# Two decoder blocks in one kernel: the program's first loads and last stores cut into pieces

## The reference

```python
def rms_norm(x, g):
    xf = x.astype(jnp.float32)
    y = xf * lax.rsqrt(jnp.mean(xf * xf, axis=-1, keepdims=True) + NORM_EPS)
    return (y * g.astype(jnp.float32)).astype(x.dtype)

def swiglu(x, w1, w2):
    gu = x @ w1
    g, u = gu[..., :D_FF], gu[..., D_FF:]          # D_FF = 2816
    return (jax.nn.silu(g) * u) @ w2

x = x + 0.5 * swiglu(rms_norm(x, ffn1_norm[0]), ffn1_w1[0], ffn1_w2[0])   # the first phase
...
h = h + swiglu_2(rmsnorm(h, ffn_norm[1]), ffn_w_gu[1], ffn_w_down[1])     # the last feed-forward
return rmsnorm(h, final_norm)                                             # the last norm
```

## Time and profile before

| | |
|---|---|
| Median of 3 runs | 2128.18 us (2127.81 to 2129.77) |
| Profiled execution: device time, span of its instructions | 2129.35 us, 2127.5 us |
| PE busy | 2040.4 us (96%) |
| DVE, ACT, POOL busy | 1236.3 us (58%), 1008.9 us (47%), 239.9 us (11%) |
| HBM traffic | 354 MB, mean 166 GB/s |
| Chain that ended last | PE 80%, DVE 9%, ACT 4% |

### The profile page before, as it was taken

The page is one execution under the profiler, slowest core; times in us unless marked ns, Lnnn a source line. Parts: engine busy times, 40 slices in busy tenths (PEclk is TensorE's granted clock), DMA queues, the critical chain, the costliest instruction groups (busy, mean ns, idle before and its releaser), DMA issues.

```text
span 2127.5 us, 26438 instructions
## 1 busy us (share of the span) xinstructions
PE 2040.4 (96%) x9866; PEld 1683.7 (79%) x9866; DVE 1236.3 (58%) x1361; ACT 1008.9 (47%) x1270; POOL 239.9 (11%) x354
## 2 busy tenths in 40 slices
PE   6999988999999999988999999999999999999997
PEld 5888876778888888876778887778778888788886
DVE  4545659965545545659965555555555545446453
ACT  4344664445445344664445444544545344454442
POOL 1000069000000000069000002111100000000000
PEclk9999998999999999998999999999999999999999
DMA  6554532455555554542455554444435554415552
GB/s 221 202 192 170 196 142 85 166 183 181 194 179 185 201 193 169 197 142 87 164 183 191 195 179 158 145 145 145 139 119 186 189 193 163 158 60 208 187 187 79
DMA packets 53617, 354.14 MB, mean 166 GB/s; under 512 B 7584, under 2 KB 8224, under 8 KB 11680
## 3 DMA queue, kind: packets, MB, share of 16 engines
q1 hardware_dynamic: 53536, 353.04, 46.7%
HBM read 351.97 MB, written 1.05 MB: 166 GB/s over the span
## 4 chain that ended last, share of the span: by engine, by line
PE 80%; DVE 9%; ACT 4%; DVEq 2%; issue 2%; POOL 1%; POOLq 1%; DMA 1%; ACTq 0%; SPq 0%
PE psum L1706 56%; PE psum L1757 17%; DVE wlo L972 3%; DVE arena L1160 2%; ACT whi L545 2%; DVEq L1154 2%; PE psum L1774 1%; PE psum L1830 1%; PE psum L2122 1%; PE psum L2143 1%; DMA raw<-w_stream 1%; PE psum L2129 1%; PE psum L1718 1%; PE psum L1878 0%; DVE arena L1171 0%
## 5 line engine op out<-in xcount | busy, mean ns | idle before, releaser
L972 DVE TENSOR_TENSOR wlo<-raw,whi 128x2048 fp32r<-128x2048 f32 x325 | 744.1, 2292 | 448.3 <-ACT whi L545 447.9
L1706 PE MATMUL psum<-whi,xTh 128*128 128x512 f32 (+1 forms) x1936 | 769.1, 397 | 22.2 <-DVE xTl L979 11.6
L1706 PE MATMUL psum<-wlo,xTh 128*128 128x512 f32 (+1 forms) x1936 | 753.3, 389 | 0.0
L1706 PE MATMUL psum<-whi,xTl 128*128 128x512 f32 (+1 forms) x1936 | 753.1, 389 | 0.0
L545 ACT ACTIVATE whi<-raw 128x2048 fp32r<-128x2048 f32 x325 | 621.1, 1916 | 264.2 <-PE psum L1757 151.3
L1706 PEld LDWEIGHTS psum<-whi,xTh 128*128 128x128 f32 x1936 | 367.0, 190 | 100.0 <-DVE wlo L1529 10.3
L1706 PEld LDWEIGHTS psum<-whi,xTl 128*128 128x128 f32 x1936 | 367.0, 190 | 76.4
L1706 PEld LDWEIGHTS psum<-wlo,xTh 128*128 128x128 f32 x1936 | 367.7, 190 | 69.4
L1757 PE MATMUL psum<-whi,braT 128*128 128x512 f32 x1056 | 337.8, 390 | 1.0 <-DVE braT L1098 1.0
L1757 PEld LDWEIGHTS psum<-whi,braT 128*128 128x128 f32 x1056 | 198.3, 188 | 42.4 <-DVE braT L1098 1.3
L1757 PE MATMUL psum<-wlo,braT 128*128 128x512 f32 x528 | 205.5, 389 | 0.0
(11 more groups left out here) (227 smaller groups left out, 1482.2 us busy)
## 6 DMA issues: line engine op xcount, KB each, us to landing
raw<-w_stream SPq DMA_DIRECT2D x327, 1024.0 KB, 4.8
bias<-chunks SPq DMA_DIRECT2D x18, 256.0 KB, 5.0
x<-x_in SPq DMA_DIRECT2D x1, 1024.0 KB, 5.1
arena<-gate_w SPq DMA_DIRECT2D x2, 512.0 KB, 5.3
arena<-fins SPq DMA_DIRECT2D x2, 512.0 KB, 5.8
out<-x SPq DMA_DIRECT2D x1, 1024.0 KB, 4.0
con<-consts SPq DMA_DIRECT2D x1, 720.0 KB, 11.9
vec<-vecs SPq DMA_DIRECT2D x2, 94.5 KB, 4.4
```

Source lines behind the costliest of these rows:

```text
L972: TT(wlo[:, r], raw[:, r], whi[:, r].bitcast(F32), ALU.subtract).then_inc(lo_done, 1)
L1706: ins = pe.matmul(dst(rb), s(kt)[:, rows], w[:, r, at_:at_ + cols], start=start and n == 0 and k == 0, stop=stop and n == len(kts) - 1 and ...
```

## The change

The diff has two halves.

At the start: SP no longer issues the positions and the gain; ACT issues them on its own queue, as its first two instructions. x is loaded in two column halves, slot 0 in four quarters of 512 columns, with its own semaphore each, in the order first constants, x half 0, quarter 0, x half 1, quarters 1 to 3, slot 1, slot 2. ACT copies (`first_hi`) and DVE subtracts (`first_lo`) quarter by quarter, and `norm_hi` and `norm_lo` of the first tiles stand behind the first quarter. PE waits for slot 0 quarter by quarter. The two sines on ACT stand behind the silu of unit 0 in the first feed-forward. POOL makes the bf16 masks after the first norm factors instead of before.

At the end: the last feed-forward also runs `last_units`, in an order of its own that completes row block 0 first. DVE adds row block 0's quarters, multiplies x by the final gain into `d_x` at once, then does row block 1. ACT squares quarter by quarter, POOL makes the factor of one row block at a time, and the last scaling is one multiply by a per-token factor: the left half of each row block on ACT, which also stores it, the right half on DVE, stored by SP. The output leaves in four stores.

```diff
@@ sync @@
-            sp.dma_start(posi[:], positions).then_inc(pos_in, 16)
+            def x_half(c):
+                sp.dma_start(x[:, :, c * W:(c + 1) * W], x_in.rearrange("(r p) c -> p r c", p=P)[:, :, c * W:(c + 1) * W]).then_inc(x_loaded[c], 16)
+            def first_piece(n):
+                sp.dma_start(raw[:, 0, n * W:(n + 1) * W], w_stream[0, :, n * W:(n + 1) * W]).then_inc(piece_in[n], 16)
             sp.dma_start(con[:, 0:FIRST], consts[:, 0:FIRST]).then_inc(con_in, 16)
-            sp.dma_start(x[:], x_in.rearrange("(r p) c -> p r c", p=P)).then_inc(x_loaded, 16)
-            sp.dma_start(gain[:], gains[0]).then_inc(gain_in, 16)
-            for s in range(3):
+            x_half(0)
+            first_piece(0)
+            x_half(1)
+            for n in range(1, 4):
+                first_piece(n)
+            for s in range(1, 3):
                 sp.dma_start(raw[:, s], w_stream[s]).then_inc(loaded[s], 16)
...
-            sp.wait_ge(x_done, phases[-1][1].x + 8)
-            sp.dma_start(out.rearrange("(r p) c -> p r c", p=P), x[:]).then_inc(stored, 16)
-            sp.wait_ge(stored, 16)
+            for rb in range(RB):
+                sp.wait_ge(out_dve, rb + 1)
+                sp.dma_start(out[rb * P:(rb + 1) * P, W:], x[:, rb, W:]).then_inc(stored, 16)
+            sp.wait_ge(stored, 16 * 2 * RB)
@@ scalar @@
+            def first_hi(n):
+                act.wait_ge(piece_in[n], 16)
+                ins = act.activation(whi[:, 0, n * W:(n + 1) * W], raw[:, 0, n * W:(n + 1) * W], ACT.Copy)
+                if n == 3:
+                    ins.then_inc(hi_done, 1)
+                else:
+                    ins.then_inc(piece_hi, 1)
...
             def ffn(b):
                 if not b.early:
+                    first_hi(0)
                     norm_hi(b, 0)
+                    for n in range(1, 4):
+                        first_hi(n)
+                    act.wait_ge(loaded[1], 16)
+                    act.activation(whi[:, 1], raw[:, 1], ACT.Copy).then_inc(hi_done, 1)
                 norm_hi(b, 1)
...
                 silu(0)
+                if not b.early:
+                    act.wait_ge(trig_pool, 1)
+                    act.activation(msin[:], ang[:, 0].rearrange("p (r n) -> p r n", r=RB), ACT.Sin)
+                    act.activation(mcos[:], ang[:, 1].rearrange("p (r n) -> p r n", r=RB), ACT.Sin).then_inc(trig_act, 1)
                 with act.Fori(1, UNITS - 1) as j:
...
-            act.wait_ge(trig_pool, 1)
-            act.activation(msin[:], ang[:, 0].rearrange("p (r n) -> p r n", r=RB), ACT.Sin)
-            act.activation(mcos[:], ang[:, 1].rearrange("p (r n) -> p r n", r=RB), ACT.Sin).then_inc(trig_act, 1)
-            for s in range(2):
-                act.wait_ge(loaded[s], 16)
-                act.activation(whi[:, s], raw[:, s], ACT.Copy).then_inc(hi_done, 1)
+            def fin(b):
+                def square(rb, c):
+                    act.wait_ge(x_done, b.x + 2 * rb + c + 1)
+                    n = 2 * rb + c
+                    ins = act.activation(junk[:, 0:W], x[:, rb, c * W:(c + 1) * W], ACT.Square, accum_out=ss8[:, n:n + 1])
+                    if c:
+                        ins.then_inc(ss_done, 1)
+                    act.drain()
+                def out_left(rb):
+                    act.wait_ge(r_done, b.norm + rb + 1)
+                    act.wait_ge(xg_done, 4 + 2 * rb + 2)
+                    act.activation(x[:, rb, 0:W], d_x[:, rb, 0:W], ACT.Copy, scale=rs[:, rb:rb + 1]).then_inc(out_act, 1)
+                    act.wait_ge(out_act, rb + 1)
+                    act.dma_start(out[rb * P:(rb + 1) * P, 0:W], x[:, rb, 0:W]).then_inc(stored, 16)
+                square(0, 0)
+                square(0, 1)
+                square(1, 0)
+                out_left(0)
+                square(1, 1)
+                out_left(1)
+            act.dma_start(posi[:], positions).then_inc(pos_in, 16)
+            act.dma_start(gain[:], gains[0]).then_inc(gain_in, 16)
@@ vector @@
             def ffn(b):
                 if not b.early:
+                    first_lo(0)
                     norm_lo(b, 0)
+                    dve.wait_ge(x_loaded[1], 16)
+                    dve.sem_inc(x_done, 2)
+                    for n in range(1, 4):
+                        first_lo(n)
+                    dve.wait_ge(hi_done, 2)
+                    TT(wlo[:, 1], raw[:, 1], whi[:, 1].bitcast(F32), ALU.subtract).then_inc(lo_done, 1)
                 norm_lo(b, 1)
...
+                def last_rows(c, rb):
+                    dve.drain()
+                    cols = slice(c * W, (c + 1) * W)
+                    TT(d_x[:, rb, cols], x[:, rb, cols], gfin[:, cols], ALU.mult).then_inc(xg_done, 1)
+                if not b.next:
+                    dve.wait_ge(fin_in, 32)
+                    residual(0, b.ffn_scale, ready, ((0, 0), (1, 0)))
+                    last_rows(0, 0)
+                    last_rows(1, 0)
+                    for c in range(2):
+                        residual(0, b.ffn_scale, ready, ((c, 1),))
+                        last_rows(c, 1)
+                    return
...
             def fin(b):
-                dve.wait_ge(r_done, b.norm + 1)
-                dve.wait_ge(fin_in, 32)
-                for c in range(2):
-                    for rb in range(RB):
-                        xs = x[:, rb, c * W:(c + 1) * W]
-                        STT(xs, xs, rs[:, rb:rb + 1], gfin[:, c * W:(c + 1) * W], ALU.mult, ALU.mult).then_inc(x_done, 1)
+                for rb in range(RB):
+                    dve.wait_ge(r_done, b.norm + rb + 1)
+                    dve.drain()
+                    TS(x[:, rb, W:], d_x[:, rb, W:], rs[:, rb:rb + 1], None, ALU.mult).then_inc(out_dve, 1)
@@ gpsimd @@
+            def fin(b):
+                for rb in range(RB):
+                    wait(ss_done, b.norm * 2 + rb + 1)
+                    r = rs[:, rb:rb + 1]
+                    TT(r, ss8[:, 2 * rb:2 * rb + 1], ss8[:, 2 * rb + 1:2 * rb + 2], ALU.add)
+                    pool.drain()
+                    TS(r, r, 1.0 / D, EPS, ALU.mult, ALU.add)
+                    pool.drain()
+                    TT(r, r, mhalf[:, 0:1], ALU.pow).then_inc(r_done, 1)
@@ tensor: use @@
-                pe.wait_ge(lo_done, b.slot + more + (i + 1))
+                first = isinstance(i, int) and isinstance(more, int) and b.slot + more + i == 0
+                if not first:
+                    pe.wait_ge(lo_done, b.slot + more + (i + 1))
                 for n, (kt, at_) in enumerate(kts):
+                    if first and n < 3:
+                        pe.wait_ge(piece_lo, n + 1)
+                    elif first:
+                        pe.wait_ge(lo_done, 1)
@@ tensor: last_units @@
+                    if not b.next:
+                        down_block(before, j - 1, 0, 0)
+                        down_block(before, j - 1, 1, 0)
+                        pe.wait_ge(h_row, b.ffn * UNITS + UNITS)
+                        turn_h(j)
+                        down_block(before, j - 1, 0, 1)
+                        down_block(last, j, 0, 0, stop=True).then_inc(ffn_out, 1)
+                        down_block(last, j, 1, 0, stop=True).then_inc(ffn_out, 1)
+                        down_block(before, j - 1, 1, 1).then_inc(slot_used, 1)
+                        down_block(last, j, 0, 1, stop=True).then_inc(ffn_out, 1)
+                        down_block(last, j, 1, 1, stop=True).then_inc(slot_used, 1)
+                        return
```

More of the change, by code:

```diff
@@ L382, in h_of @@
         def h_of(b, j, part):
-            t0 = 2 if b.next and isinstance(j, int) and j == UNITS - 1 else 0
+            t0 = 2 if isinstance(j, int) and j == UNITS - 1 else 0
             return braT[:, part, t0:t0 + 2]
@@ L1759, in down_block, with down @@
                     return ins
-                def down(i, j, more=0, first=False, last=False):
+                def down(i, j, more=0, first=False):
                     for c in range(2):
                         for rb in range(RB):
-                            ins = down_block(i, j, c, rb, more, first, last)
-                            if last and not (c == 1 and rb == 1):
-                                ins.then_inc(ffn_out, 1)
+                            ins = down_block(i, j, c, rb, more, first)
                     ins.then_inc(slot_used, 1)
@@ L1809, in ffn @@
                 unit(1, first=True)
-                with pe.Fori(2, UNITS - 1 if b.next else UNITS) as j:
+                with pe.Fori(2, UNITS - 1) as j:
                     unit(j)
-                if b.next:
-                    last_units()
-                else:
-                    pe.wait_ge(h_row, b.ffn * UNITS + UNITS)
-                    turn_h(UNITS - 1)
-                    down(3 * UNITS - 1, UNITS - 1, last=True)
+                last_units()
             def turn(b, plan, name, parts, at_=None):
```

44 lines of the change are left out of this document (29 added, 15 removed).

## The result

The changed kernel takes 2112.84 us (median of 6 runs, 2112.17 to 2114.13); the kernel before, run beside it, 2128.19 us (6 runs, 2127.51 to 2129.77). The ratio is 0.9927, 95% interval 0.9917 to 0.9938: 15.35 us less, where 15.7 and 2112.5 us were forecast. The profiled execution took 2112.89 us with a span of 2111.1; that is its kernel's median, while the profiled execution before (2129.35 us, granted clock 0.980) stands 1.16 above its own.

A forecast was written before the change was run, and what follows sets the result against it. The prediction saw a long run of matmuls on PE with two uncovered ends. Start 10.5 plus end 5.2 gave 15.7 us, so 2128.18 - 15.7 = 2112.5 us, range 2108.0 to 2119.2.

The forecast's parts named there:

- the start: From the kernel's start to the first matmul on slot 2: gain 10.5 us, bounds 7 and 12.5.
- the end: Last unit, final norm and stores: gain 5.2 us, bounds 3.5 and 6.2.
- The mark: First matmul on slot 2, after which every unit repeats: forecast to move from 33.98 to 23.5 us.
- the two chains: Two paths to the first matmul on slot 2: PE's own at 23.5, slot 1 and 2 splits at 23.2; a tie.
- POOL's masks and the tables are wanted by the mixer near 200 us: nothing: POOL's mask casts and the sine tables in the first feed-forward: moving them later was priced at nothing.
- The sines: Two sines moved behind ACT's first silu: priced at nothing; without the cover of ACT's idle time, 1.3 us a unit.
- The reload rival: Uncovered table reload in the first feed-forward's loop: 1.28 us in each of nine passes, 11.5 in all, 2124.0 us; chance 0.04.
- The low clock: PE's first matmuls at the start: twelve at 1.2 GHz, 0.42 us apart, 5.1 us.
- Twelve matmuls less at the low clock would give 2.4 more: Bound on the start: twelve fewer slow matmuls on PE give 2.4 us, twelve more take 2.4.
- Serial fixed cost: Loads at the start: six pieces each add 2 us before the next, slot 1 8 us later, 2120.5 us; chance 0.05.
- Late clock: Waits between pieces keep PE at 1.2 GHz through slots 0 and 1: 7.2 us lost, 2119.7 us; chance 0.08.
- Slower: Low clock continues past the start; 79 more slow matmuls eat the gain, two units give 2141 us; chance 0.03.

The follow-up runs named there:

- start_only: The changed kernel with the norm, the last unit and the store put back as they were before: 2118.9 us, ratio 0.9955.
- masks_late: The changed kernel with GpSimd's mask casts moved to the head of the mixer's program; they ran at the same time as before: 2112.68 us.
- warm: The changed kernel with small fp32 products on TensorE while it waits, eight before the first transposes and four behind: 2116.66 us, ratio 0.9947.
- all_five: The changed kernel with the edits of `order`, `warm` and `masks_mixer`, and the last square ahead of the left half: 2111.12 us, ratio 0.9918.
- order: The changed kernel with slot 1 split in halves, slot 2's split ahead of the squares, second turned rows ahead of slot 1: 2112.13 us, ratio 0.9922.
- end_only: The kernel before with only the norm, last unit and store as in the changed kernel: 2122.14 us, ratio 0.9973.
- sines_first: The changed kernel with the two sines put back ahead of the first quarter on ScalarE: 2119.32 us, ratio 0.9956.
- masks_mixer: The changed kernel with GpSimd's two casts moved into the first mixer, behind its first waits: 2113.78 us, ratio 0.9933.
- whole_loads: The changed kernel with x and slot 0 each loaded by one DMA, work still in quarters: 2115.45 us, ratio 0.9937.

## Why the prediction was right, and where its terms were off

The mechanism held: two uncovered ends, independent of each other, the middle untouched. The total was within 0.4 us of the measured one, and that is in part luck: the start gave 1.15 us less than forecast, the end 0.8 more.

**The start: 9.35 us, 10.5 forecast.** The mark was forecast at 23.5 with the two chains tied at 23.5 and 23.2. They are still nearly tied (24.40 and 24.59), 0.9 and 1.4 us later. Arrivals: x half 0 at 5.2 (5.4 forecast), quarter 0 at 6.7 (6.2), x half 1 at 8.3 (7.9), quarter 1 at 9.85 (8.7), the last quarter at 11.1 (10.4), slot 1 at 13.66 (13.0). What was mis-sized is the transfer of the pieces in the middle: 314 GB/s were taken from a stretch of 0.19 MB, and the queue moved 235 between 5.20 and 6.70 us and over 400 from 8.3 on. Slot 1 then came 2.5 us behind the last quarter, as forecast (2.6). SyncE's slow issues are not the cause: in `start_only` its three issues of quarters took 2.47 us instead of 1.71 and slot 1 was issued at 5.14 instead of 4.38, and yet it landed earlier, at 13.08.

On TensorE's side the first matmul was at 9.14 (8.7), and tile 4 at 18.85 (18.0), by slot 1's lateness; 24 matmuls take it to 24.40.

On the data side slot 1's 0.66 and the cast's 0.94 come to 1.6, and 0.2 less for the copies and squares (5.74 us from slot 1's landing to slot 2's split; 5.95 summed). The cast is the mis-priced step: "POOL's masks and the tables are wanted by the mixer near 200 us: nothing" is true of who waits for their result, and false of who shares their time. In the kernel before the casts ran at 16.77 and 18.38, long before slot 2's split, and its low parts at 31.43 took 4.50 for two. The exclusion could have been read there already, from the other side: the identity's cast took 1.65 us beside VectorE's low part (0.29 us in `masks_late`, with VectorE idle). The bounds of the start, 7 and 12.5 us, have no working of their own: the 2.4 us either way that stand before them would give 8.1 and 12.9.

**The sines: nothing, as priced.** The reload rival is out: silu's table serves the sines too (from 24.64 to the mixer's at 206.49 there is no load), so no 1.28 us falls into any unit.

**The low clock: twelve matmuls, as forecast.** But the step "Twelve matmuls less at the low clock would give 2.4 more" was wrong as a statement on this kernel. With them alone taken away the mark came 1.4 us later (`warm`). With the data chain freed as well it came 3.1 earlier (`all_five`), where the data chain alone had given 0.8 (`order`). That difference, 2.3, is close to the 2.4, but it is there only once the other chain is out of the way. A bound worked out for one of two tied chains isn't a bound for the kernel.

**The end: 5.96 us, 5.2 forecast.** Last residual 1.26 us sooner behind the last up projection (1.06 worked out). From it to the last store's issue 4.27 us (4.3), with the last square 0.65 late behind the left quarter and its issue (0.5). From that issue to the span's end 2.92 us, where 3.5 was taken: ScalarE's last quarter landed in 2.5 us, not in 3.1; the first one, alone in the queue for most of its time, in 2.0, and both of SyncE's in 2.0. So the two last stores cost each other 0.5 us at most. (Of the blocks of the unit before, two lie behind the last `turn_h`, not three as the prediction says; its sum uses only the one that follows at once.)

**The middle: nothing.** The 1.1 us by which the two traces differ there are what single executions vary by, and the forecast had set that apart (1.17 us between the profiled execution and the median). From the mark to silu's table load near 1600 us, where all kernels do the same work but for sines and casts, the fourteen traces take 1577.1 to 1580.8 us: the kernel before 1578.9, `end_only`, with the same start, 1580.0, the changed kernel 1577.9. They follow no order of how early the mark is. The 1.8 us of `sines_first` and much of what `all_five` lost lie within this.

**The rivals.** Serial fixed cost: out, slot 1 landed 0.7 us later than forecast, not 8. Late clock: out here, though `warm` shows the thing itself, with a wait of 2.29 us behind a full clock. Slower: no sign of it.

## What to carry to other kernels

Where two chains arrive together, price an edit by both: removing a cost from one gives only what the other is behind, and a faster TensorE can pay its gain back in clock by waiting longer (here 2.29 us of waiting, eight matmuls at half speed). When an instruction is moved because "nobody wants its result", look at what runs beside it at its new place. And a difference of one or two microseconds between two single traces of 2100 is not yet an effect: the same 1580 us of work varied by 3.7 here, so hold it against the medians before you explain it.

## What the runs showed of the hardware that was not expected

- VectorE's fp32 subtraction of two SBUF operands and GpSimd's cast from SBUF take turns by whole instructions: 3.23 us instead of 2.29 beside one cast, 6.49 for two beside three casts, 3.13 instead of 1.25 for the cast that waits.
- SyncE's issues vary in length: the first ones 0.4 to 0.46 us each, the last quarter's 0.69, two whole slots 1.27, and the three quarters' together 1.54 us (`masks_mixer`) to 2.47 (`start_only`). Why isn't shown, and slot 1's landing doesn't follow them.
- The same bytes arrive more slowly in pieces: 235 GB/s between 5.20 and 6.70 us against 391 (`whole_loads`), slot 1 at 13.66 against 11.7.
- The table that is loaded for silu serves the sine too: no load at 26.66. The other way round it doesn't: with the sines first, silu has a load of its own at 28.86 (`sines_first`).
- The number of matmuls at 1.2 GHz behind nearly the same start (first product at 9.14 to 9.40) was twelve in the changed kernel, eight in `start_only`, none where small products ran ahead of it (`warm`, `all_five`).
- Two quarter stores (256 KB) from two queues at once landed in 2.0 and 2.5 us, where one store of 1 MB took 4.0.
